# One product of three passes, laid one pass at a time between the small products of a matrix inverse

## What is computed

```
y_mla = causal_block_attention(q, k, v)                      # 8 heads x 64 = channels 0..511
...
a = where(strict, (kb @ k^T) * decay, 0) + eye(64)           # per chunk of 64 tokens and head
sol = triangular_solve(a, rhs, lower=True, unit_diagonal=True)
...                                                          # recurrence over 4 chunks
y = concatenate([y_mla, o.reshape(b, s, 512)], axis=-1)      # attention | gated delta rule
return y @ w_out                                             # (256 x 1024) @ (1024 x 1024)
```

## Time and profile before

| | us |
|---|---|
| median of 3 runs | 1070.44 |
| lowest, highest | 1068.08, 1070.94 |
| the profiled execution, its own time | 1070.33 |
| its span in the trace | 1068.4 |
| PE busy, of the span | 1050.0 (98%) |
| PEld busy | 963.3 (90%) |
| DVE busy | 810.2 (76%) |
| ACT busy | 563.9 (53%) |
| POOL busy | 46.5 (4%) |

### The profile page before, as it was taken

How to read it: one execution, slowest core, us unless ns; L and a number is a source line. 1 busy time by engine, 2 the same in 40 slices (tenths; PEclk the granted TensorE clock), 3 DMA queues, 4 the chain that set the end, 5 groups by cost and what they waited for, 6 DMA issues and landing times.

```text
span 1068.4 us, 19234 instructions
## 1 busy us (share of the span) xinstructions
PE 1050.0 (98%) x8325; PEld 963.3 (90%) x8325; DVE 810.2 (76%) x1071; ACT 563.9 (53%) x695; POOL 46.5 (4%) x32
## 2 busy tenths in 40 slices
PE   8999999999899999999999999999999999999998
PEld 7999987898778899998789999878888889999986
DVE  5877789899663687778988767898665647766797
ACT  6644455585674554445645444564665436444451
POOL 1000000110073000000000000000000000000000
PEclk9999999999899999999999999999999999999999
DMA  9765556563001666555656655666655556565551
GB/s 304 237 188 171 194 197 186 167 198 119 1 5 33 207 198 192 169 193 197 197 158 200 195 177 178 198 202 225 189 173 176 170 156 214 173 196 178 179 195 40
DMA packets 127214, 184.91 MB, mean 173 GB/s; under 512 B 4221, under 2 KB 101738, under 8 KB 127002
## 3 DMA queue, kind: packets, MB, share of 16 engines
q1 hardware_dynamic: 126384, 181.85, 53.2%
q0 software_dynamic: 448, 1.71, 0.5%
q10 hardware_dynamic: 298, 0.12, 0.0%
HBM read 182.62 MB, written 1.05 MB: 172 GB/s over the span
## 4 chain that ended last, share of the span: by engine, by line
PE 79%; DVE 15%; issue 4%; ACT 2%; DMA 1%; SPq 0%; ACTq 0%; DVEq 0%
PE banks L1516 22%; PE banks L1518 22%; PE banks L1517 22%; DVE wlo L960 3%; DVE arena L1032 2%; DVE rounded L1040 2%; PE banks L1959 2%; DVE arena L1033 1%; DVE raw L1034 1%; PE banks L1678 1%; PE banks L1679 1%; PE banks L1677 1%; DVE wlo L1042 1%; PE banks L1594 1%; PE banks L1595 1%
## 5 line engine op out<-in xcount | busy, mean ns | idle before, releaser
L952 DVE TENSOR_TENSOR wlo<-raw,whi 128x2048 fp32r<-128x2048 f32 (+1 forms) x142 | 321.1, 2271 | 106.0 <-ACT whi L500 105.7
L1516 PE MATMUL banks<-xTh,whi 128*128 128x256 f32 x1392 | 394.6, 284 | 2.1 <-DVE wlo L1175 1.9
L500 ACT ACTIVATE whi<-raw 128x2048 fp32r<-128x2048 f32 (+1 forms) x170 | 311.0, 1841 | 160.5 <-PE banks L1518 144.3
L1517 PE MATMUL banks<-xTl,whi 128*128 128x256 f32 x1392 | 393.9, 283 | 0.0
L1518 PE MATMUL banks<-xTh,wlo 128*128 128x256 f32 x1392 | 393.9, 283 | 0.0
L1516 PEld LDWEIGHTS banks<-xTh,whi 128*128 128x128 f32 x1392 | 267.2, 192 | 2.8 <-issue 1.7
L1517 PEld LDWEIGHTS banks<-xTl,whi 128*128 128x128 f32 x1392 | 267.2, 192 | 0.0
L1518 PEld LDWEIGHTS banks<-xTh,wlo 128*128 128x128 f32 x1392 | 267.2, 192 | 0.0
L1516 PE MATMUL banks<-whi,hTh 128*128 128x512 f32 (+1 forms) x192 | 77.7, 405 | 1.5 <-DVE wlo L1042 1.5
L1518 PE MATMUL banks<-whi,hTl 128*128 128x512 f32 (+1 forms) x192 | 74.6, 389 | 0.0
L1517 PE MATMUL banks<-wlo,hTh 128*128 128x512 f32 (+1 forms) x192 | 74.5, 388 | 0.0
(11 more groups left out here) (289 smaller groups left out, 1530.8 us busy)
## 6 DMA issues: line engine op xcount, KB each, us to landing
raw<-in_ffn_w_down SPq DMA_DIRECT2D x44, 1024.0 KB, 4.9
raw<-in_ffn_w_gate SPq DMA_DIRECT2D x43, 1024.0 KB, 5.4
raw<-in_ffn_w_up SPq DMA_DIRECT2D x43, 1024.0 KB, 5.4
raw<-in_sg_w_in SPq DMA_DIRECT2D x16, 1024.0 KB, 5.5
raw<-in_ab_w_in SPq DMA_DIRECT2D x8, 1024.0 KB, 5.2
raw<-in_sg_w_out SPq DMA_DIRECT2D x8, 1024.0 KB, 4.8
raw<-in_ab_w_out SPq DMA_DIRECT2D x4, 1024.0 KB, 4.9
raw<-in_ab_w_in SPq DMA_DIRECT2D x2, 832.0 KB, 4.4
```

The costliest lines, as they stand in the source:

```text
L500: A(whi[:, j % SLOTS, 0:n], raw[:, j % RAW_SLOTS, 0:n], ACT.Copy).then_inc(S("hi_ready"), 1)
L952: TT(wlo[:, j % RAW_SLOTS, 0:n], raw[:, j % RAW_SLOTS, 0:n], whi[:, j % SLOTS, 0:n].bitcast(f32), ALU.subtract).then_inc(S("lo_ready"), 1)
L1516: mm(out_ap, lh, rh, start=first, stop=False)
L1517: mm(out_ap, lh, rl, start=False, stop=False)
```

## The change

`early` gets a third argument, the pass, and issues one matmul in place of three. The loop calls it three times for each product, at three places. Of the odd product, pass 0 stands behind `d_next(n, 0)`, pass 1 behind `dt_next(n, 0)`, pass 2 behind `d_next(n, 1)`. Of the even one, pass 0 stands ahead of `dt_next(n, 1)`, pass 1 behind it, pass 2 behind `m1(n + 1, 1)`. The three passes of the last product, (1, 3), stay together. Sums, banks, waits and the number of matmuls stay; a wait that stands ahead of a pass is now taken where that pass is.

```diff
-            def early(t, kk):
+            def early(t, kk, part):
                 j = b + 12 + kk // 2
-                wh, wl = slot(j)
-                if t == 0 and kk % 2 == 0:
+                wh, wl = (w[:, kk % 2, 512:1024] for w in slot(j))
+                if t == 0 and kk % 2 == 0 and part == 0:
                     begin(j)
...
+                left, right = ((hTh, wh), (hTh, wl), (hTl, wh))[part]
+                last = mm(B[EARLY_BANK[t]][:], left[:, kk, tok], right, start=kk == 0 and part == 0,
+                          stop=kk == 3 and part == 2, skip_group_check=True)
...
             for n in range(4):
+                odd, even = divmod(2 * n - 1, 4), divmod(2 * n, 4)
...
                 d_next(n, 0)
                 if n:
+                    early(*odd, 0)
                     pe.wait_ge(S("dt_merged"), 2 * n)
...
                 dt_next(n, 0)
                 if n:
-                    early(*divmod(2 * n - 1, 4))
+                    early(*odd, 1)
...
                 d_next(n, 1)
+                if n:
+                    early(*odd, 2)
                 pe.wait_ge(S("d_merged"), 2 * n + 1)
                 m1(n + 1, 0)
                 pe.wait_ge(S("dt_merged"), 2 * n + 1)
                 if n == 0:
                     pe.wait_ge(S("yT_lo"), 4)
+                early(*even, 0)
                 dt_next(n, 1)
-                early(*divmod(2 * n, 4))
+                early(*even, 1)
                 pe.wait_ge(S("d_merged"), 2 * n + 2)
                 m1(n + 1, 1)
-            early(1, 3)
+                early(*even, 2)
+            for part in range(3):
+                early(1, 3, part)
```

More of the change, by code:

```diff
@@ L2031, in y_transposes @@
                         last.then_inc(S("yT_sums"), 1)
-            def early(t, kk):
+            def early(t, kk, part):
                 j = b + 12 + kk // 2
-                wh, wl = slot(j)
-                if t == 0 and kk % 2 == 0:
+                wh, wl = (w[:, kk % 2, 512:1024] for w in slot(j))
+                if t == 0 and kk % 2 == 0 and part == 0:
                     begin(j)
-                last = split_mm(B[EARLY_BANK[t]][:], hTh[:, kk, P * t:P * t + P], hTl[:, kk, P * t:P * t + P],
-                                wh[:, kk % 2, 512:1024], wl[:, kk % 2, 512:1024], kk == 0, kk == 3)
-                if kk == 3:
+                tok = slice(P * t, P * t + P)
+                left, right = ((hTh, wh), (hTh, wl), (hTl, wh))[part]
+                last = mm(B[EARLY_BANK[t]][:], left[:, kk, tok], right, start=kk == 0 and part == 0,
+                          stop=kk == 3 and part == 2, skip_group_check=True)
+                if kk == 3 and part == 2:
                     last.then_inc(S("early_sums"), 1)
```

## The result

| | before | after |
|---|---|---|
| median of 22 runs, us | 1069.98 | 1072.45 |
| lowest, highest | 1067.95, 1072.89 | 1069.49, 1073.86 |
| profiled execution, own time (span) | 1070.33 (1068.4) | 1073.86 (1072.0) |
| stage of the inverse in it | 28.14 | 31.28 |

The ratio of after to before is 1.0019, with a 95% interval of 1.0010 to 1.0027: 0.19% slower, 2.0 us (1.1 to 2.9). The medians of all runs differ by 2.5 us. The forecast was 1072.7 us, 2.4 us over the profiled execution of before.

The account below looks back on a forecast made before the run. PE was taken to bound the kernel, busy 98% of the span. Levels of 20.18 us after less 17.79 us before, with 1.51 us of stalls given back, add 2.39 us to 1070.33 us: 1072.7 us, range 1070.3 to 1074.8 us.

Parts of the forecast that it names:

- That PE alone ends the stage, and copies are late for nobody: Levels of the inverse: the chain of waits never leaves PE, DVE waits 13.0 us for it, no new copy wait.
- That the stalls are edges of instruction blocks: Levels: PE stalls every 127 matmuls, where a block of its instructions ends; least time between blocks 3.4 to 3.8 us.
- 0.35 us for a cluster: Levels: each row of full-array passes between small matmuls costs 0.35 us over its passes; ends 0.20 and 0.41 us.
- 19 steps and the last cluster: Levels after: one pass and a group of 32, 1.05 us, 19 times, 19.95 us; last cluster's fourth pass adds 0.23 us.
- That all stalls are absorbed: Levels: 127 matmuls now take 4.04 us, over a block's 3.4 to 3.8 us, so 1.51 us of stalls is given back.
- the first rival: Levels: stalls stay or come back elsewhere while clusters cost 4.0 us; +3.9 us, 1074.2 us; chance 0.20.
- The first pass for nothing: Pass 0 of (0, 0), ahead of dt_next(0, 1), lies in the 0.92 us stall and costs nothing, by 0.05 us.
- The sum: Levels: 20.18 us of work after less 17.79 us before, +2.39 us, all reaching the end at 1072.7 us; chance 0.62.
- The second rival: Levels: stalls are waits for copies, so passes fill them at no cost; -2.1 us, 1068.2 us; chance 0.08.
- The third: Behind the levels: slack takes up the added time, 0 to +1 us, 1070.8 us; chance 0.10.

Follow-up runs that it names:

- The shift of the program: Kernel before with 64 small matmuls more ahead of the stage (groups m1(0, 0) and m1(0, 1) issued twice): stage 28.96 us, time 1070.50 us.
- the run with all products behind: Kernel before with all eight products of three passes in one cluster behind the levels: stage 32.58 us, time 1074.47 us.
- the halved columns: Both kernels with 256 columns in place of 512 in each pass: stage 28.99 us before, 28.56 us after; time 1068.26 and 1070.98 us.
- the second execution: Each kernel, unchanged, profiled once more: stage 29.46 us before, 30.96 us after; time 1071.96 and 1073.31 us.
- without the pass: Changed kernel with pass 0 of (0, 0) moved back behind dt_next(0, 1), beside pass 1: stage 31.19 us, time 1073.02 us.
- the five clusters: Changed kernel with its 24 passes in five clusters of 4 or 5: stage 29.18 us, median 1070.13 us, ratio to the kernel before 1.0004.

## Why the prediction was right

- *That PE alone ends the stage, and copies are late for nobody*: right. The levels have no wait for a copy in either kernel.
- *That the stalls are edges of instruction blocks*: right. The shift of the program and the run with all products behind show it, and the halved columns show that a block's pace, not PE's work, set the stage before.
- *0.35 us for a cluster*: right. Pass and group step by 1.06 us, not 1.05 us, which is 0.16 us over 19 of them.
- *19 steps and the last cluster*: 20.28 + 1.12 us against 19.95 + 1.13 us. The rest of the 0.33 us is the stall of 0.17 us.
- *That all stalls are absorbed*: nearly. PE's 4.04 us for a block is a mean. The block from 314.34 to 318.14 us (by count) has one cluster less than its neighbours and is 3.64 us of work, and it took 3.81 us; in the second execution the same block took 3.81 us too. So 0.17 us of the 1.51 us stayed, and the first rival, that stalls stay, was right to this extent and no more. The 3.39 us that the prediction gives to each of three blocks from 309.24 to 319.42 us is a mean as well: by count they took 3.88, 2.95 and 3.36 us. The second had next to no stall at 2.95 us, and the packet for it began 0.7 us behind the edge before and not 1.1, so 3.4 us is the least only from stall to stall. There the runs have 3.4 to 4.05 us.
- *The first pass for nothing*: right in its kind. In the first execution the block itself came 0.4 us later into the stage than before, which no pass caused: without the pass it came at 5.33 us too, against 5.08 us in the earlier trace rows (309.24 - 304.16).
- *The sum*: the stage was forecast at 28.14 + 2.39 = 30.5 us and came out at 31.28 and 30.96 us, 0.4 to 0.8 us more. Of the 0.75 us in the first execution, 0.4 us lie ahead of pass 1 of (0, 0), where the block came late, 0.16 us in the steps and 0.17 us in the stall that stayed; so the last cluster begins at 331.07 us and not at 329.8 us, 0.56 us of that being the later start of the stage. That the time still agrees owes something to chance: the execution from which I read had a quick stage, 1.3 us under the second. By the means of two, 31.1 - 28.8 = 2.3 us were added, and the runs say 2.0 us (1.1 to 2.9).
- *The second rival, passes that fill gaps for free*: out, since each cluster paid its 0.35 us. *The third, slack behind the stage*: not seen; from the stage's end to the last matmul both traces agree within 0.2 us, and of the difference of the spans, 3.6 us, the stage has 3.1 us and the part ahead of it, where the program is the same, 0.6 us (304.72 against 304.16 us at the stage's start).

## What to carry to other kernels

Before laying a large product in pieces between small ones, look whether the gaps are waits: here the copies waited for PE, and the stalls came each 127 matmuls, by the count of instructions; work laid between fills such a stall and doesn't shorten the block. Going from matmuls in quarters of the array to full ones and back cost 0.35 us, by the number of clusters and not by their length. In this stretch, which was bound by its instructions, 2.6 us of work under the pace of the blocks cost nothing that could be seen, and the same work over it cost all of its 2.4 to 2.7 us. And where a stage is bound so, read it from more than one execution before taking a duration as its least.

## What I had not expected of the hardware

The time from one block of instructions to the next scatters in the same program, from 3.4 to 4.05 us from stall to stall. The trace's record of the instruction queue shows where most of this lies. Of the kernel before, the block that took 3.39 us (305.85 to 309.24) had its packet begin 1.06 us behind the edge and last 0.93 us, and the stall ended 1.41 us after the packet. The block that took 3.77 us (319.42 to 323.19) has 1.11, 1.34 and 1.32 us: the packet itself took longer. The slowest, 4.05 us in the second execution, has 1.69, 0.92 and 1.44 us: its packet began late. From stall to stall no packet begins earlier than 1.06 us behind the edge before, so a block is fetched only once PE has entered the one before it. Why a packet is slow or late stays open.

The clock fell for one stretch just ahead of the stage in nine of the eleven traces and not in the other two. The same two stretches of 7 us, columns as in the earlier trace rows with PEclk third from the end, of the kernel before and then of the one with half the columns, which differ only behind them:

```profile
277.00:283.90 6.90, 4.99 (x37) 3.65 (x36) 6.51 (x15) 4.27 (x14) 0.00 (x0) 1.00 0.00 0
283.90:290.70 6.80, 6.28 (x85) 5.85 (x85) 2.07 (x4) 3.92 (x12) 0.00 (x0) 0.50 0.01 2
```

```profile
277.00:283.90 6.90, 5.03 (x38) 3.69 (x36) 6.54 (x15) 4.29 (x14) 0.00 (x0) 1.00 0.00 0
283.90:290.70 6.80, 6.25 (x116) 5.83 (x118) 4.61 (x10) 4.70 (x16) 0.00 (x0) 1.00 0.01 2
```

In the first of them PE was busy for 4.99 and 5.03 us, and nothing in these rows tells the two apart; the second ran at the lower level in one and at the upper in the other. With the lower level (1.2 GHz) the stage begins at 304.16 us, with the upper one (2.4 GHz) at 301.27 us. The runs fall in two groups by it: of the changed kernel's 22 runs, the six with a mean clock of 1.000 have a median of 1069.9 us, the 14 at 0.997 or less 1072.7 us; the two at 0.998 lie between, at 1071.0 and 1071.2 us. Of the 17 runs of the kernel before that were made beside the five clusters, ten at 1.000 have 1068.1 us and seven at 0.997 or less 1071.3 us. Within a group the change costs 1.8 and 1.4 us, as far as runs made at different times can be set side by side. This lottery of 3 us is wider than the change itself; why it falls one way or the other stays open.
